# Split fp32r products for the expert keys and for two gathering blocks whose dots are fetched from memory, and for most value tiles

## The chip, the cores and the metric

The kernel runs on one core of one Trainium2 chip. The metric is the device time of a run in microseconds. Runs of the kernel before took 2939.55 to 2944.12 us, the median of three is 2941.18 us.

## What is computed

One encoder layer on 1024 tokens of width 1024: a mixer (a bidirectional gated recurrence and a convolution group between two projections), then a retrieval over 16384 single-neuron experts, then a last normalisation. The change concerns the retrieval:

```python
def _peer(h, wq, keys1, keys2, u_tab, v_tab):
    q = (h @ wq).reshape(nb, L, PEER_HEADS, PEER_DKEY)
    ...
    s1 = jnp.einsum('blhd,kd->blhk', q1, keys1)
    s2 = jnp.einsum('blhd,kd->blhk', q2, keys2)
    v1, i1 = lax.top_k(s1, PEER_TOPK)
    v2, i2 = lax.top_k(s2, PEER_TOPK)
    ...
    w = jax.nn.softmax(sc, axis=-1)
    ...
        u_sel = u_tab[ex]
        act = jax.nn.gelu(jnp.einsum('td,tjd->tj', hx, u_sel))
        coef = (wx * act)
        return jnp.einsum('tj,tjd->td', coef, v_tab[ex])
```

Each token has 8 heads x 16 = 128 experts e. For each it needs the dot of its h with row e of u, the gelu of that, times a softmax weight, times row e of V, summed. u and V have 16384 rows of 1024 floats (4 KB) each.

## The kernel before, in words

The program runs `step1`, `front`, `step4` (all up to the residual before the retrieval) and then `step6`, which is the retrieval and the ending. The token blocks of 128 are treated in two ways.

**Gathering blocks** 0 to 3 (`SPARSE = 4`). When a block is ranked (its 128 experts per token are known, `row[b]`), GpSimd orders one indirect DMA per expert place j (line 1657): 128 partitions each fetch their own 4 KB row of u or V into one of 8 ring slots (`RING`). `fetch(i)` waits until row i-8 has been taken. VectorE takes each: for u a product with h of that block that sums into `dot[b][:, j]` (line 2166; h stands in PSUM, `ph`), for V a multiply-add into `hB` (line 2180). The function `wanted(m)` gives the order, `sparse_by(n)` says how many rows are to be taken by tile n of u (in tenths per tile) and `sparse_by_v(n)` by tile n of V. The first 40 V rows of block 0 go another way, the side: fetched into two slots of their own and added on TensorE through a diagonal matrix (line 1752, `SIDE_ROWS`).

**Dense blocks** 4 to 7 (512 tokens). For these TensorE multiplies with all of u, tile by tile of 128 experts: `u_tile(n)` (line 1705) makes 8 plain fp32 products of 128x512, first for 16 tiles of the query weights (`QT`), then for 128 tiles of u. ScalarE copies or applies gelu (lines 1865, 1857) and stores to memory (`m.g`). Meanwhile VectorE ranks the blocks (`pick_step`, `ranked_key`), makes one-hot matrices (`one_hots`, lines 2139 to 2142), ScalarE their further parts (line 1910), TensorE multiplies them into a table of weights (line 1742), and ScalarE copies that out (line 1892) and stores it. Below this stretch, from the first query tile to the last tile of u, is called the u stage.

**V stage.** For 128 tiles of V, VectorE makes the product of g and the weights (`product_of`, lines 2198 and 2199), six tiles ahead, and TensorE multiplies 8 plain fp32 products per tile into all 8 banks of PSUM (line 1809). VectorE does the V rows of the gathering blocks in between. Then the sums are turned, the residual added, normalised and stored.

Every engine works through its own instructions in order, so a wait holds all that stands behind it. SP issues the loads of u and V tiles, weights and scores. Split products are used before already: `project` (lines 340, 341, 344) multiplies in fp32r with high and low parts of both sides, hi x hi, hi x lo, lo x hi; ScalarE rounds (line 324) and GpSimd subtracts (line 328).

## Time and profile before

| | |
|---|---|
| median of runs | 2941.18 us |
| profiled execution's own time | 2928.15 us, span 2926.1 us |
| TensorE busy | 2779.2 us (95%) |
| VectorE busy | 2238.6 us (77%) |
| GpSimd busy | 1263.6 us (43%) |
| ScalarE busy | 870.2 us (30%) |
| moved by DMA | 911.47 MB, of it 536.94 MB by the indirect gathers |

The profile comes from one execution. PE is TensorE's matmul part, PEld its loading of weights, DVE VectorE, ACT ScalarE, POOL GpSimd, SP the engine that issues loads. A "q" behind a name means the engine's sequencer. L1657 is line 1657 of the kernel. Time in which an engine waits is shown with what ended the wait. Matmuls overlap, so the mean time of one is longer than the distance between two; the distance is what counts. In a row of busy time by stretch the five engines stand as PE, PEld, DVE, ACT, POOL, each with its number of instructions.

### The profile page before, as it was taken

How to read it: one execution, taken by the hardware profiler on the slowest of the kernel's cores; microseconds unless marked ns; L12 is line 12 of the kernel's file. 1: busy time of each engine (PE TensorE's matmuls, PEld its weight loads, DVE VectorE, ACT ScalarE, POOL GpSimd, SP SyncE). 2: the span in 40 equal slices, each digit the busy share in tenths (PEclk: the TensorE clock that was granted, in tenths of full speed). 3: DMA queues.
4: the chain of work that ended last, by engine and by line, in shares of the span. 5: the costliest groups of instructions: out<-in, count | busy, mean ns of one | idle time of the engine just before them, and what ended most of it. 6: DMA issues, size and time to landing. Idle time of an engine off the chain costs nothing.

```text
span 2926.1 us, 31227 instructions
## 1 busy us (share of the span) xinstructions
PE 2779.2 (95%) x10124; PEld 1513.1 (52%) x10124; DVE 2238.6 (77%) x4600; ACT 870.2 (30%) x1733; POOL 1263.6 (43%) x1089
## 2 busy tenths in 40 slices
PE   6999889899999989999999999989999999999995
PEld 3677677787654434544454545534444444444442
DVE  5998566336799999999998968776776676677675
ACT  3223465333211014754664757800000000000004
POOL 1001111213354554444444445564666566656661
PEclk9999999999999999999999999999999999999997
DMA  5641101234499999999999999999999999999994
GB/s 204 252 173 40 48 30 47 85 135 123 161 406 388 388 379 338 399 383 369 393 360 365 369 400 414 416 407 390 405 402 405 407 397 405 398 402 401 402 393 180
DMA packets 284595, 911.47 MB, mean 311 GB/s; under 512 B 26001, under 2 KB 73361, under 8 KB 277137
## 3 DMA queue, kind: packets, MB, share of 16 engines
q0 software_dynamic: 147456, 536.94, 47.1%
q1 hardware_dynamic: 99632, 297.56, 27.1%
q10 hardware_dynamic: 37344, 74.98, 6.6%
q8 instruction: 81, 1.33, 0.2%
q14 instruction: 82, 0.66, 0.1%
HBM read 826.01 MB, written 83.36 MB: 311 GB/s over the span
## 4 chain that ended last, share of the span: by engine, by line
PE 23%; DMA 20%; DVE 19%; POOL 9%; issue 4%; DVEq 1%; ACT 1%; SPq 1%; ACTq 0%; PEldq 0%; POOLq 0%
DMA s_slot<-in_v,s_row 17%; PE s_pu L1705 16%; DVE s_slot L2166 10%; POOL s_slot L1657 9%; PE s_pw L1742 2%; DMA s_slot<-in_u,s_row 2%; DVE s_hB L2180 2%; PE s_ps L1752 1%; DMA s_wr<-s_w 1%; PE s_pu L340 1%; PE s_pu L341 1%; PE s_pu L344 1%; DVE pk_key L1364 1%; PE s_ps L1826 1%; DVE pk_key L1355 1%
## 5 line engine op out<-in xcount | busy, mean ns | idle before, releaser
L1705 PE MATMUL s_pu<-s_hn,s_ut 128*128 128x512 f32 x2304 | 1007.2, 593 | 4.3 <-ACT s_gst L1857 3.0
L1657 POOL DMA_INDIRECT s_slot<-in_v,s_row x512 | 638.5, 1247 | 372.6 <-DVE s_hB L2180 257.2
L2180 DVE SCALAR_TENSOR_TENSOR s_hB<-s_slot,s_dot,s_hB 128x1024 f32<-128x1024 f32 x469 | 593.3, 1284 | 254.2 <-DMA s_slot<-in_v,s_row 236.3
L1657 POOL DMA_INDIRECT s_slot<-in_u,s_row x512 | 504.6, 986 | 599.0 <-DVE s_slot L2166 521.1
L1705 PEld LDWEIGHTS s_pu<-s_hn,s_ut 128*128 128x128 f32 x2304 | 433.2, 190 | 530.0 <-issue 527.0
L2166 DVE SCALAR_TENSOR_TENSOR s_slot<-s_slot,s_ps 128x1024 f32<-128x1024 f32 x512 | 608.9, 1219 | 80.9 <-DMA s_slot<-in_u,s_row 60.3
L1809 PE MATMUL s_ps<-s_ct,s_vt 128*128 128x512 f32 x1024 | 460.3, 592 | 0.0
L1809 PEld LDWEIGHTS s_ps<-s_ct,s_vt 128*128 128x128 f32 x1024 | 194.6, 190 | 245.0 <-issue 245.0
L1910 ACT ACTIVATE s_hotw<-s_hot,s_rest 128x128 bf16<-128x128 bf16 x1024 | 308.5, 423 | 28.5 <-ACT s_gst L1857 23.7
L1989 ACT ACTIVATE s_sq<-y 128x512 f32<-128x512 f32 x16 | 8.9, 626 | 921.1 <-DVE y L2253 921.1
L1809 PE MATMUL s_pw<-s_ct,s_vt 128*128 128x512 f32 x512 | 246.0, 603 | 24.8 <-DMA s_vt<-in_v_tiles 15.6
L1809 PE MATMUL s_pu<-s_ct,s_vt 128*128 128x512 f32 x512 | 242.6, 596 | 0.0
L328 POOL TENSOR_TENSOR w_lo<-s2w_raw,w_hi 128x1024 fp32r<-128x1024 f32 x15 | 38.0, 2533 | 414.3 <-ACT w_hi L324 414.3
L340 PE MATMUL s_ps<-hn_hi,w_hi 128*128 128x512 f32 x464 | 189.0, 407 | 8.5 <-DVE hn_lo L280 8.0
L1857 ACT ACTIVATE s_gst<-s_pu 128x512 f32<-128x512 f32 x120 | 71.6, 597 | 403.7 <-PE s_pu L1705 403.1
L341 PE MATMUL s_ps<-hn_lo,w_hi 128*128 128x512 f32 x464 | 184.1, 397 | 0.0
L1809 PEld LDWEIGHTS s_pw<-s_ct,s_vt 128*128 128x128 f32 x512 | 97.5, 192 | 151.2 <-issue 129.3
L1809 PEld LDWEIGHTS s_pu<-s_ct,s_vt 128*128 128x128 f32 x512 | 98.7, 193 | 125.3 <-issue 125.3
L1028 DVE SCALAR_TENSOR_TENSOR s_work<-s_hp,cols,s_work 128x1024 f32<-128x1024 f32 x111 | 146.6, 1320 | 8.0 <-issue 0.4
L344 PE MATMUL s_ps<-hn_hi,w_lo 128*128 128x512 f32 x464 | 144.9, 394 | 0.0
L1892 ACT ACTIVATE s_wb<-s_pw 128x512 f32<-128x512 f32 x128 | 124.5, 1074 | 4.0 <-PE s_pw L1742 3.6
L1742 PEld LDWEIGHTS s_pw<-s_hotw,s_hot 128*128 128x128 bf16 x1536 | 93.1, 97 | 37.7 <-issue 37.3
(326 smaller groups left out, 2861.2 us busy)
## 6 DMA issues: line engine op xcount, KB each, us to landing
s_ut<-in_u_tiles SPq DMA_DIRECT2D x128, 512.0 KB, 7.4
s_vt<-in_v_tiles SPq DMA_DIRECT2D x32, 2048.0 KB, 16.9
s_g<-s_gst ACTq DMA_DIRECT2D x120, 256.0 KB, 7.0
s_w<-s_wb ACTq DMA_DIRECT2D x15, 2048.0 KB, 11.7
s_wr<-s_w SPq DMA_DIRECT2D x16, 1920.0 KB, 27.6
s_gr<-s_g SPq DMA_DIRECT2D x60, 512.0 KB, 26.7
s_ada<-in_ada SPq DMA_DIRECT2D x48, 512.0 KB, 6.2
s2w_raw<-in_w_in SPq DMA_DIRECT2D x26, 512.0 KB, 3.6
```

Source lines behind the costliest of these rows:

```text
L340: pe.matmul(out[:, c], w_hi[:, k, :], x_hi[:, h, k, :], start=(k == first), stop=False)
L341: pe.matmul(out[:, c], w_hi[:, k, :], x_lo[:, h, k, :], start=False, stop=False)
L344: mm = pe.matmul(out[:, c], w_lo[:, k, :], x_hi[:, h, k, :], start=False, stop=(k == last))
L1028: dve.scalar_tensor_tensor(dst, hp[:, k:k + T], cw[:, c, k:k + 1], work[:, :], ALU.mult, ALU.add)
L1657: pool.indirect_dma_start(out=slot[s][:, :], out_offset=None, in_=io[kind], in_offset=bass.IndirectOffsetOnAxis(ap=row[b][:, j:j + 1], axi ...
L1705: mm = pe.matmul(pu[:, n % 2, :], ut[n % UR][:, k, :], hn[:, k, :], start=(k == 0), stop=(k == DC - 1))
L1742: mm = pe.matmul(pw[:, unit % 2, j * P:(j + 1) * P], hot2[n % 2][:, q, :, t], hotw[n % 2][x][:, q, :, t], start=(x == 0), stop=(x == 2))
L1809: mm = pe.matmul(bank(c), vt[n // VG % VR][:, n % VG, c * P:(c + 1) * P], ct[:, n % CR, :], start=(n == 0), stop=(n == KEYS - 1))
L1892: act.activation(wb[chunk % 2][:, :, t:t + 4].rearrange("p k t -> p t k"), pw[:, unit % 2, :].rearrange("p (t k) -> p t k", t=4), ACT.Copy)\
L1910: o = act.activation(hotw[n % 2][1 + x][:, q, :, t], hot1[n % 2][:, q, :, t], ACT.Copy, scale=rest[:, x, 8 * r + i:8 * r + i + 1])
L2166: dve.scalar_tensor_tensor(s, s, 1.0, ph[:, :], ALU.mult, ALU.mult, accum_out=dot[b][:, j:j + 1]).then_inc(taken, 1)
L2180: dve.scalar_tensor_tensor(y, s, dot[b][:, j:j + 1], y, ALU.mult, ALU.add).then_inc(taken, 1)
```

## The change

1. **Dense tokens.** u and the query weights come as slices of 128x512 (one chunk k of the width for four tiles at once, `GROUP = 4`), 288 in all, through 5 buffers. ScalarE rounds a slice to `raw_hi` (3 buffers), and GpSimd (three of four slices) or VectorE (the fourth) subtracts to `raw_lo` in place. TensorE makes three fp32r products for each of four key banks. The dense tokens' h is kept as high and low parts too.
2. **Blocks 2 and 3** no longer gather u. With each slice of u, TensorE also multiplies their tokens (stationary) with all 512 keys of the slice, into two token banks. ScalarE copies these out through one buffer, `y_found`, and stores them in memory: 16384 dots for each token. When u is done, GpSimd fetches for each expert place the one dot per token by an indirect DMA of 4 bytes per partition (`find`), eight to a batch; ScalarE applies gelu to a batch, VectorE multiplies by the softmax weight.
3. **Gathering.** The order is now u of blocks 0 and 1, V of blocks 0 and 1, V of blocks 2 and 3: 768 rows in place of 984 and 40. `SIDE` and its TensorE work go. u products read h from SBUF (`hB`) and not from PSUM. One buffer for scores in place of two.
4. **V.** Of the 128 tiles 90 are split: ScalarE rounds the product and the tile, VectorE subtracts both, TensorE makes 24 fp32r products per tile. The other 38 stay plain.
5. The planner's numbers (`sparse_by`, `HOT_AT`) change, and h of the four gathering blocks is kept in two halves of 256 tokens (`ho_hi`, `ho_lo`, `project_gathering`).

```diff
+def project_gathering(pe, m, out, w_hi, w_lo, ks=range(DC)):
+
+    for k in ks:
+        x_hi, x_lo = m.ho_hi[:, :, k, :], m.ho_lo[:, :, k, :]
+        pe.matmul(pairs(out), w_hi[:, k, :], x_hi, start=(k == 0), stop=False)
+        pe.matmul(pairs(out), w_hi[:, k, :], x_lo, start=False, stop=False)
+        mm = pe.matmul(pairs(out), w_lo[:, k, :], x_hi, start=False, stop=(k == DC - 1))
     return mm
 
...
-RANKED = (0, 1, 2, 4, 5, 6, 3, 7)
+OWN_U = 2
+RANKED = (0, 1, 2, 4, 5, 6, 7, 3)
...
 RING = 8
-SIDE = 2
-SIDE_ROWS = 40
...
+GROUP = 4
+QG = QT // GROUP
+GROUPS = QG + KEYS // GROUP
+SLICES = DC * GROUPS
+RAW, ROUNDED = 5, 3
 KEPT = 8
...
-HOT_AT, HOT_TILES = (28, 54, 79, 101), (20, 20, 18, 17)
-SIDE_AT, SIDE_TILES = 26, 74
+HOT_AT, HOT_TILES = (28, 50, 72, 94), (19, 19, 19, 19)
+PLAIN_V = 120
+V_PARTS = [n for n in range(PLAIN_V) if n % 4]
+FOUND = 8
...
+def wanted(m):
+
+    if m < OWN_U * P:
+        return "u", m // P, m % P
+    j, b = divmod(m - OWN_U * P, 2)
+    return "v", 2 * (j // P) + b, j % P
+
+
+def slice_at(n):
+    return 2 * (n + QT)
+
+
+def split_by_dve(i):
+    return i % 4 == 0
 
...
-        tenths += 42 if t < 2 else 33 if t < 30 else 35 if t < 93 else 43 if t < 118 else 39
+        tenths += 22 if t < 0 else 37 if t < 28 else 25 if t < 93 else 42 if t < 114 else 50
...
+                for i in (slice_at(n), slice_at(n) + 1):
+                    if i >= RAW:
+                        sp.wait_ge(slice_done, i - RAW + 1)
+                    else:
+                        sp.wait_ge(wq.used, 2 * PH + (1 if i < 4 else 2))
+                    g, k = divmod(i, DC)
+                    sp.dma_start(raw[i % RAW][:, :], io["wq_groups"][g, k] if g < QG else io["u_groups"][g - QG, k])\
+                        .then_inc(raw_in[i % RAW], 16)
                 for i in range(MADE_PICKS, len(RANKED)):
...
+            def find(x, j):
+                if j == 0 and x >= 4:
+                    pool.wait_ge(found_used, x - 3)
+                e, c = found_column(x, j)
+                pool.indirect_dma_start(out=dot[OWN_U + e][:, c:c + 1], out_offset=None, in_=m.found[e],
+                                        in_offset=bass.IndirectOffsetOnAxis(ap=found_at[e][:, c:c + 1], axis=0))\
+                    .then_inc(found_in[x % 4], 16)
+
+            def remainder(i):
+                pool.wait_ge(raw_rounded, i + 1)
+                pool.tensor_tensor(raw_lo[i % RAW][:, :], raw[i % RAW][:, :], raw_hi[i % ROUNDED][:, :].bitcast(F32),
+                                   ALU.subtract).then_inc(raw_split[0], 1)
 
...
+                for i in (slice_at(n) + 2, slice_at(n) + 3):
+                    if i < SLICES and not split_by_dve(i):
+                        remainder(i)
+                    until = sparse_by(n + 1) if i % 2 else (asked + sparse_by(n + 1)) // 2
+                    for i in range(asked, until):
+                        fetch(i)
+                        asked = i + 1
+            for i in range(asked, V_FIRST):
+                fetch(i)
+            pool.wait_ge(y_stored, 16 * 2 * (KEYS // GROUP))
+            pool.wait_ge(found_ready, 2)
+            for x in range(2):
+                for j in range(FOUND):
+                    find(x, j)
+            for i in range(V_FIRST, SPARSE_OPS):
+                x, j = divmod(i - V_FIRST + 2 * FOUND, FOUND)
+                if x < 2 * P // FOUND:
+                    find(x, j)
                 fetch(i)
 
...
-            def u_tile(n):
-                i = n + QT
-                pe.wait_ge(u_in[n % UR], 16 * (i // UR + 1))
-                if i >= 2:
-                    pe.wait_ge(gelu_done, i - 1)
-                for k in range(DC):
-                    mm = pe.matmul(pu[:, n % 2, :], ut[n % UR][:, k, :], hn[:, k, :],
-                                   start=(k == 0), stop=(k == DC - 1))
-                mm.then_inc(u_done, 1)
+            def u_slice(i):
+                g, k = divmod(i, DC)
+                pe.wait_ge(raw_split[split_by_dve(i)], splits_before(i) + 1)
+                hi, lo = raw_hi[i % ROUNDED], raw_lo[i % RAW]
+                places = banks_of(g)
+                for kind, j in places:
+                    first, last = k == 0, k == DC - 1
+                    if first and g and (kind, j) in banks_of(g - 1):
+                        pe.wait_ge(emptied, emptied_before(g - 1) + banks_of(g - 1).index((kind, j)) + 1)
+                    if kind == "k":
+                        c = slice(j * P, (j + 1) * P)
+                        pe.matmul(key_bank[j], hi[:, c], m.hn_hi[:, 1, k, :], start=first, stop=False)
+                        pe.matmul(key_bank[j], hi[:, c], m.hn_lo[:, 1, k, :], start=False, stop=False)
+                        mm = pe.matmul(key_bank[j], lo[:, c], m.hn_hi[:, 1, k, :], start=False, stop=last)
+                    else:
+                        t = slice(j * P, (j + 1) * P)
+                        pe.matmul(token_bank[j], m.ho_hi[:, 1, k, t], hi[:, :], start=first, stop=False)
+                        pe.matmul(token_bank[j], m.ho_lo[:, 1, k, t], hi[:, :], start=False, stop=False)
+                        mm = pe.matmul(token_bank[j], m.ho_hi[:, 1, k, t], lo[:, :], start=False, stop=last)
+                    if (kind, j) == places[-1]:
+                        mm.then_inc(slice_done, 1)
+                    elif last:
+                        mm.then_inc(filled, 1)
...
+                if n in V_PARTS:
+                    x = V_PARTS.index(n)
+                    pe.wait_ge(v_split, x + 1)
+                    pe.wait_ge(ct_split, x + 1)
+                    hi, lo = v_hi[x % 2], v_lo[n // VG % VR]
+                    x_hi, x_lo = ct_hi[x % 4][:, :], ct_lo[:, n % CR, :]
+                    for c in range(DC):
+                        d = slice(c * P, (c + 1) * P)
+                        pe.matmul(bank(c), hi[:, d], x_hi, start=False, stop=False)
+                        pe.matmul(bank(c), hi[:, d], x_lo, start=False, stop=False)
+                        mm = pe.matmul(bank(c), lo[:, n % VG, d], x_hi, start=False, stop=False)
+                    mm.then_inc(v_done, 1)
+                    continue
...
+            def round_slice(i):
+                act.wait_ge(raw_in[i % RAW], 16 * (i // RAW + 1))
+                if i >= ROUNDED:
+                    act.wait_ge(slice_done, i - ROUNDED + 1)
+                act.activation(raw_hi[i % ROUNDED][:, :], raw[i % RAW][:, :], ACT.Copy).then_inc(raw_rounded, 1)
+
+            def empty_group(g):
+                t = g - QG
+                storing = []
+                for x, (kind, j) in enumerate(banks_of(g)):
+                    if x == len(banks_of(g)) - 1:
+                        act.wait_ge(slice_done, DC * (g + 1))
+                    else:
+                        act.wait_ge(filled, filled_before(g) + x + 1)
+                    if kind == "t":
+                        if 2 * t + j:
+                            act.wait_ge(y_stored, 16 * (2 * t + j))
+                        act.activation(y_found[:, :], token_bank[j], ACT.Copy).then_inc(emptied, 1)
+                        act.wait_ge(emptied, emptied_before(g) + x + 1)
+                        act.dma_start(m.found[j].rearrange("(t k) o -> t (k o)", t=P)[:, t * HALF:(t + 1) * HALF], y_found[:, :])\
+                           .then_inc(y_stored, 16)
+                    elif t < 0:
+                        if g:
+                            act.wait_ge(sd_made, GROUP * (g - 1) + j + 1)
+                        act.activation(qst[j][:, :], key_bank[j], ACT.Copy).then_inc(emptied, 1)
+                    elif GROUP * t + j >= KEYS - KEPT:
+                        act.activation(ct[:, (GROUP * t + j) % CR, :], key_bank[j], ACT.Gelu).then_inc(emptied, 1)
+                    else:
+                        if t:
+                            act.wait_ge(g_stored[j], 16 * t)
...
+            def round_product(x):
+                n = V_PARTS[x]
+                act.wait_ge(product, n + 1)
+                if x >= 4:
+                    act.wait_ge(v_done, V_PARTS[x - 4] + 1)
+                act.activation(ct_hi[x % 4][:, :], ct[:, n % CR, :], ACT.Copy).then_inc(ct_rounded, 1)
+
+            def round_tile(x):
+                n = V_PARTS[x]
+                act.wait_ge(v_in[n // VG % VR], 16 * (n // (VG * VR) + 1))
+                if x >= 2:
+                    act.wait_ge(v_done, V_PARTS[x - 2] + 1)
+                else:
+                    act.wait_ge(slice_done, SLICES)
+                act.activation(v_hi[x % 2][:, :], vt[n // VG % VR][:, n % VG, :], ACT.Copy).then_inc(v_rounded, 1)
+
+            def gelu_found(x):
+                e, c = found_column(x, 0)
+                act.wait_ge(found_in[x % 4], 16 * FOUND * (x // 4 + 1))
+                act.activation(dot[OWN_U + e][:, c:c + FOUND], dot[OWN_U + e][:, c:c + FOUND], ACT.Gelu).then_inc(found_used, 1)
+
...
-                    dve.scalar_tensor_tensor(s, s, 1.0, ph[:, :], ALU.mult, ALU.mult,
+                    dve.scalar_tensor_tensor(s, s, 1.0, hB[b][:, :], ALU.mult, ALU.mult,
...
+            def remainder(i):
+                dve.wait_ge(raw_rounded, i + 1)
+                dve.tensor_tensor(raw_lo[i % RAW][:, :], raw[i % RAW][:, :], raw_hi[i % ROUNDED][:, :].bitcast(F32),
+                                  ALU.subtract).then_inc(raw_split[1], 1)
+
```

## Rows read from the trace of the kernel before

**Rows 1.** Busy time by stretch: us, five engines in turn, clock, DMA share, GB/s
```profile
772.00:1966.00 1194.00, 1168.80 (x4140) 569.62 (x4140) 1059.61 (x2907) 552.58 (x1379) 582.97 (x583) 0.99 0.99 381
1966.00:2868.00 902.00, 885.47 (x2044) 390.19 (x2045) 640.73 (x686) 0.00 (x0) 559.58 (x441) 0.99 1.03 401
2868.00:2926.10 58.10, 24.43 (x69) 12.45 (x67) 30.42 (x39) 30.49 (x48) 0.57 (x1) 0.73 0.32 123
```

**Rows 2.** Chain of waits: shares of the span by engine; two pieces (start, us)
```profile
PE 23%; DMA 20%; DVE 19%; POOL 9%; issue 4%; DVEq 1%; ACT 1%; SPq 1%; ACTq 0%; PEldq 0%; POOLq 0%
...
1423.62 1.77 PE s_ps L1752 x4
...
1742.34 27.47 PE s_pu L1705 x64
```

**Rows 3.** Group of instructions on TensorE: shape, count, busy us, mean ns, idle before
```profile
L1705 PE MATMUL s_pu<-s_hn,s_ut 128*128 128x512 f32 x2304 | 1007.2, 593 | 4.3 <-ACT s_gst L1857 3.0 <-ACT s_hB L1952 1.1 <-DMA s_ut<-in_u_tiles 0.2
```

**Rows 4.** Instructions in order of time, TensorE in the query projection: start, us
```profile
689.98 0.39 PE L340 MATMUL s_pu<-hn_hi,w_hi 128*128 128x512 f32 x1
...
697.46 0.39 PE L340 MATMUL s_pu<-hn_hi,w_hi 128*128 128x512 f32 x1
```

**Rows 5.** Instructions in order of time, ScalarE in a tile with one-hots
```profile
1811.33 0.60 ACT L1857 ACTIVATE s_gst<-s_pu 128x512 f32<-128x512 f32 x1 [0.63 <-PE s_pu L1705]
...
1812.38 4.82 ACT L1910 ACTIVATE s_hotw<-s_hot,s_rest 128x128 bf16<-128x128 bf16 x16 [0.46 <-ACT s_gst L1857]
1817.08 1.94 ACT L1892 ACTIVATE s_wb<-s_pw 128x512 f32<-128x512 f32 x2
1819.63 0.60 ACT L1857 ACTIVATE s_gst<-s_pu 128x512 f32<-128x512 f32 x1 [0.61 <-PE s_pu L1705]
```

**Rows 6.** Groups on GpSimd in the V stage and in the u stage, and landings
```profile
L1657 POOL DMA_INDIRECT s_slot<-in_v,s_row x441 | 560.1, 1270 | 345.5 <-DVE s_hB L2180 255.0 <-issue 90.6
...
L1657 POOL DMA_INDIRECT s_slot<-in_u,s_row x512 | 504.6, 986 | 599.0 <-DVE s_slot L2166 521.1 <-issue 42.8 <-DVE s_row L2093 35.1
L1657 POOL DMA_INDIRECT s_slot<-in_v,s_row x71 | 78.3, 1103 | 27.0 <-issue 19.1 <-DVE s_slot L2166 4.8 <-DVE s_hB L2180 2.3
...
  issue: 90.6, 295
DMA to landing us min/median/max: 6.7/13.4/20.3
```

**Rows 7.** Instructions in order of time, V stage: GpSimd orders beside VectorE products
```profile
2398.79 3.67 DVE L2180 SCALAR_TENSOR_TENSOR s_hB<-s_slot,s_dot,s_hB 128x1024 f32<-128x1024 f32 x3 [0.19 <-issue]
...
2399.05 1.83 POOL L1657 DMA_INDIRECT s_slot<-in_v,s_row  x1 [0.30 <-issue]
...
2401.18 0.94 POOL L1657 DMA_INDIRECT s_slot<-in_v,s_row  x1 [0.30 <-issue]
```

**Rows 8.** Groups with two inputs in SBUF; and two VectorE products beside GpSimd
```profile
L2180 DVE SCALAR_TENSOR_TENSOR s_hB<-s_slot,s_dot,s_hB 128x1024 f32<-128x1024 f32 x469 | 593.3, 1284 | 254.2 <-DMA s_slot<-in_v,s_row 236.3 <-issue 16.5
L2199 DVE TENSOR_TENSOR s_ct<-s_gr,s_wr 128x480 f32<-128x480 f32 x120 | 78.0, 650 | 0.0
L328 POOL TENSOR_TENSOR w_lo<-s2w_raw,w_hi 128x1024 fp32r<-128x1024 f32 x15 | 38.0, 2533 | 414.3 <-ACT w_hi L324 414.3
...
259.89 6.74 DVE L1028 SCALAR_TENSOR_TENSOR s_work<-s_hp,cols,s_work 128x1024 f32<-128x1024 f32 x2
```

**Rows 9.** DMA queues from 772 to 900 us: packets, MB, share of 16 engines
```profile
q0 software_dynamic: 8573, 31.25, 63.0%
q10 hardware_dynamic: 7408, 3.68, 9.6%
```

**Rows 10.** DMA issues: count, KB each, median us to landing
```profile
s_ut<-in_u_tiles SPq DMA_DIRECT2D x128, 512.0 KB, 7.4
s_g<-s_gst ACTq DMA_DIRECT2D x120, 256.0 KB, 7.0
...
s_scores<-s_sc ACTq DMA_DIRECT2D x16, 256.0 KB, 2.3
```

422 lines of the change are left out of this document (222 added, 200 removed).

## The prediction

> **What bounds the kernel now.** I read the engines' shares on the page first (TensorE 95%), then busy time by stretch, then the chain of waits, then single instructions. The reader should see that the average hides four stages. By stretch [rows 1]: up to 772 us the front, the mixer and the first queries; 772 to 1966 (1194 us) the u stage, TensorE busy 1169; 1966 to 2868 (902 us) the V stage, TensorE busy 885; 58 us of ending. In both middle stages the DMA engines are full as well (share 0.99 and 1.03, 381 and 401 GB/s). The chain of waits [rows 2] says the same: row gathers, GpSimd, VectorE and TensorE share it. So a change must relieve TensorE and the gathers together, and neither may hand its work to an engine that becomes the next one.
>
> TensorE's prices. A plain fp32 product of 128x512 leaves two records, 1152 products giving x2304 [rows 3]; 64 records take 27.47 us [rows 2], so one product takes 0.858 us. The fp32r products of the query projection start 33 apart in 697.46 - 689.98 us [rows 4], 0.227 us each, so a split product (three of them) costs 0.680 us, 0.79 of the fp32 one.
>
> **TensorE in the u stage.** Before: 1152 products x 0.858 = 989 us; the side products 40 x 1.77 = 71 [rows 2]; the one-hot products 64 x 1.43 = 92 (a tile with them has a period of 1819.63 - 1811.33 = 8.30 us [rows 5], less 16 records x 0.429 = 6.87); the scores are what is left of the 1169 busy, 17; 25 us are idle [rows 1]. After: 32 query slices with 4 banks x 3 products = 384, and 256 slices of u with 6 banks (4 for the dense keys, 2 for blocks 2 and 3) x 3 = 4608. That is 4992 x 0.227 = 1132, plus 92 and 17: 1241 us, **+72 us**. The two extra token banks are what turns a saving into a cost. Two transposes of h fall away; the start needs the last remainder of the dense tokens instead, and I leave it at nothing.
>
> **TensorE in the V stage.** Before 1024 x 0.858 = 879. After 90 tiles split (24 x 0.227 = 5.44 us each, 490) and 38 plain (8 x 0.858 = 6.87, 261): 751 us, **-128 us**. If all the rest were hidden the kernel would win 56 us. The rest is the question.
>
> **GpSimd in the V stage.** This is my main term. The planner asks for 459 rows by the end of the u stage and there are 768, so 309 rows are left, where 442 were left before. Of these the first 53 are V rows of blocks 0 and 1. After them come 256 V rows of blocks 2 and 3, and each needs a dot that is fetched first by an indirect DMA of its own: 256 more of them. The plan hands out 309/126 = 2.45 rows per V tile. The ring lets the last of the 53 be asked for when VectorE has taken number 504, after 45/2.45 = 18 tiles, so after 18 x 5.86 + 9 (the gap at the start) = 114 us. From there GpSimd must issue 512 indirect DMAs one behind the other. One takes 1.270 us in this stage [rows 6] and 0.30 us passes between two (90.6 us over 295 [rows 6]): 1.57 us, 804 us in all. With the last landing (13.4 us [rows 6]) the stage takes 114 + 804 + 13 = **931 us**, 29 more than now, though TensorE needs only 751. A V tile then takes 2.45 x 2 x 1.57 = 7.7 us. The price varies: an indirect DMA that begins while VectorE has just begun a product with both inputs in SBUF takes 1.83 us, its neighbour 0.94 [rows 7]. The ends are 0.94 + 0.30 (512 x 1.24 = 635, stage 762) and 1.45 + 0.30 (896, stage 1023). I keep 1.57, as VectorE's load per unit of time is nearly unchanged: per V tile 2.45 x 1.28 + 0.83 for the product, and in 0.7 of the tiles the remainders of 512 and 1024 columns, 0.69 and 1.39 us by the 0.650 for 480 [rows 8], sum 5.4 us; over 7.7 us that is 70%, and now it is 641 of 902, 71% [rows 1].
>
> **DMA engines in the V stage.** Before 902 us x 401 GB/s = 362 MB. 133 rows of 0.524 MB fewer leave 292 MB, 728 us. No row shows a transfer of 4 bytes. The nearest short packets are the 512-byte ones of the scores: 9.6% of 128 us x 16 over 7408 packets [rows 9], 27 ns each; 256 x 144 x 27 ns / 16 = 61 us. The bound below is nothing, above it the time of a gather's own packets, 63.0% over 8573 [rows 9], 150 ns or 346 us. I take 61, stage 789 us: hidden behind GpSimd, but a floor for any hope that TensorE sets the end. The Trainium skill (DMA: Bandwidth & Descriptors, Bandwidth) gives a 4 KB transfer 0.68 us of engine time as its floor; 256 of these would be 174 us and make the DMA floor about 902 us. No run here shows it.
>
> **The rest of the u stage.** GpSimd orders 583 gathers in it now [rows 6] and 464 then (62 MB less; 17 MB of dots are stored), so the queues are looser. Four things are new on the path.
> 1. ScalarE rounds 288 slices, 0.6 us each, and empties a whole group of banks at once. With one store per bank it spends 1812.38 - 1811.33 = 1.05 us on each [rows 5]. The two token banks of a group go through one buffer, so the second copy waits until the store of the first has landed: 7.0 us for a store of this size now [rows 10], 2.3 us for the same size on quiet queues [rows 10]. ScalarE is in order; behind that wait stand 4.82 us of one-hot parts and 1.93 us of bank copies [rows 5], and behind them the rounding of the next slice. I follow one group from the start of its last slice: token bank 0 is full at 0.7 us and copied and sent at 1.5; bank 1 is copied from 8.5 to 9.1; the parts and copies end at 16.3, the rounding and its remainder at 18.2, while TensorE wants that slice at 4.08 + 1.43 + 8.16 + 1.43 = 15.1. So 3.1 us are lost with a store of 7 us, 0.5 with one of 3 us; I take 1.6 over 22 groups with one-hots and 0.6 us in 10 others: 40 us. Ends: 0 and 80.
> 2. GpSimd takes the remainders of 216 slices. 128x1024 took 2.53 us [rows 8], so half of it is 1.27. In the last 14 tiles five rows are planned per tile: 5 x 1.57 + 1.5 x 1.27 = 9.8 us against 8.16 of TensorE, 1.6 x 14 = 22 us. Ends 0 and 40. The 1.57 is the row of a product with both inputs in SBUF; the u products now read their h from PSUM and a gather's issue takes 0.986 beside them [rows 6], and the change moves h to SBUF.
> 3. GpSimd's subtraction and VectorE's two-input products exclude each other: two VectorE products beside two such subtractions took 6.74 us [rows 8], where one alone takes 1.28. VectorE is near full until tile 28 (busy 1060 of 1194 in the stage [rows 1]). I put 3 us here above today's idle, ends 0 and 30.
> 4. A slice is loaded four slices ahead, 16 us for a landing of 7.4 us with twice the bytes [rows 10]; covered. In the query groups it is 10.9 us less 2.5 for the splitting: covered, barely. If not, 32 slices x 1 us.
>
> The Trainium skill (GPSIMD Engine Reference, Specifications) says that GpSimd shares its SBUF interfaces with VectorE and contends with instructions of two SBUF inputs. That speaks against moving h to SBUF; without the rule the 22 us of point 2 would be 4, since 5 x 1.29 + 1.9 = 8.4. The traced 0.94 and 1.83 us agree with it.
>
> Sum: 1241 + 25 + 40 + 22 + 3 = **1331 us, +137**.
>
> **Total.** 2926.1 + 137 + 29 = 3092 us of span. Its own time is 2928.15, 2 more than the span; the median of the runs, 2941, lies 13 above that. So 3092 + 2 + 13 = 3107; since the ends of the four small terms reach further down in common than up, I say 3100.
>
> **The rivals.**
> A. GpSimd sets the V stage, as above: 3000 to 3180 us. For it: 512 orders in a row on one engine, a count that no wait can shrink.
> B. All is covered (the other side, faster). The price of an indirect DMA near 0.94 us makes GpSimd's stage 762, so the DMA floor of 789 decides; the u stage is 1241 + 25. Span 2926 + 72 - 113 = 2885, so 2900 to 2930. It decides where the mean price falls below (789 - 127)/512 = 1.29 us with the gap. Against it: VectorE's duty does not fall.
> C. Between: price 1.40 with the gap, u stage 1290: 114 + 717 + 13 = 844, so 2926 + 96 - 58 + 15 = 2979; 2945 to 3000.
> D. The chain load, round, subtract, multiply runs late in the whole u stage, because GpSimd's waits for ring slots stand ahead of subtractions: each of 144 pairs of slices 1 us late, +144 and less of point 1: 3180 to 3260. For it: the in-order queue. Against: windows of 8 us.
> E. The change doesn't do what it says, if a split product doesn't hold 0.227 us with weights changing at each: every 0.01 us is 50 + 22 us. Against it: the query stage changes weights at each one too.
>
> **How the numbers follow.** A 0.55, D 0.14 with E in it, C 0.14, B 0.14, and 0.03 for chance sums near no change. Likeliest: A, 3100 us. Leaving out the outer part of B and D the range is 2915 to 3210. A measurement can tell about 0.2%, 6 us: slower 0.80 (A, D and most of C), same 0.05, faster 0.15.
>
> **What would show it.** Right: TensorE in the V stage idle before weight loads, with waits on VectorE's products; GpSimd there without waits on ring slots, at some 1.5 us per order; V tiles of 7 to 8 us. In the u stage ScalarE's idle time before the second token copy ended by a DMA landing, once per group. Wrong: V tiles of 5.9 us; GpSimd waiting for VectorE; a u stage under 1280 us. The price of the 4-byte fetches and of the product with h in SBUF are the two that no row shows and that could undo it.

## The result, and the profile after

The changed kernel takes **3193 us** (median of 4 runs, 3185 to 3200) against 2940 us before: ratio **1.086**, 95% interval 1.083 to 1.089. The prediction was 3100 us with a range of 2915 to 3210 and 0.80 for slower, so time and sign lie inside it; the time is 3% above the forecast. The profiled execution took 3185 us, its span is 3183.2 us.

First the busy time by stretch, with the columns of [rows 1]: the u stage, two pieces of its end, and the V stage.

```profile
771.00:2186.00 1415.00, 1290.60 (x6668) 1048.47 (x6668) 1222.14 (x2625) 747.84 (x1685) 935.96 (x682) 0.97 0.84 294
1860.00:2162.00 302.00, 272.32 (x1395) 215.53 (x1394) 236.37 (x184) 149.38 (x341) 236.95 (x177) 0.99 0.93 339
2162.00:2186.00 24.00, 0.42 (x2) 0.00 (x1) 11.61 (x14) 0.98 (x2) 7.89 (x9) 0.57 1.03 409
2186.00:3140.00 954.00, 829.83 (x2768) 545.64 (x2768) 642.56 (x784) 147.44 (x216) 612.45 (x557) 0.91 0.84 301
```

The u stage grew from 1194 to 1415 us, the V stage from 902 to 954, the ending shrank from 58 to 43. In the u stage TensorE is busy 1291 us where its products at full clock make 1241; the other 124 us it idles, 24 of them in the gap ahead of V, where it waits for VectorE's first products. In the V stage it is busy 830 us where the products make 751, and idles 124 us. The DMA engines, full in [rows 1], stand at 0.84. VectorE is busy 162 us more in the u stage than before, though it works on 457 gathered rows there (256 of u, 201 of V) and not on 532 (512 and 20).

What TensorE waited for in the u stage, with total, times and longest:

```profile
PE s_ps L1795 <- DVE s_raw_lo L2309: 37.7, 15, 5.0
PE s_ps L1795 <- POOL s_raw_lo L1739: 32.4, 31, 2.3
PE s_pu L1790 <- DVE s_raw_lo L2309: 17.0, 4, 8.9
PE s_pu L1790 <- POOL s_raw_lo L1739: 8.5, 1, 8.5
PE s_ps L1795 <- ACT s_y_found L1953: 8.5, 8, 3.5
```

These are late remainders of slices, VectorE's before GpSimd's; the token banks' buffer is the last row. ScalarE's own wait for that buffer, over the whole run, is this one:

```profile
ACT s_y_found L1953 <- DMA s_found<-s_y_found: 47.5, 17, 6.9
```

The groups of VectorE in the u stage and of GpSimd in the V stage (shape, count, busy us, mean ns):

```profile
L2291 DVE SCALAR_TENSOR_TENSOR s_slot<-s_slot,s_hB 128x1024 f32<-128x1024 f32 x256 | 365.7, 1452 | 26.3 <-DMA s_slot<-in_u,s_row 13.0 <-issue 1.5
L2267 DVE TENSOR_TENSOR s_hot<-s_iota,s_keyT 128x1024 bf16<-128x1024 bf16 x64 | 63.5, 993 | 0.0
...
L1725 POOL DMA_INDIRECT s_slot<-in_v,s_row x301 | 348.9, 1159 | 224.9 <-DVE s_hB L2305 137.9 <-issue 78.6 <-DVE s_hB L2302 8.5
L1733 POOL DMA_INDIRECT s_dot<-s_found,s_found_at x256 | 263.5, 1029 | 78.0 <-issue 78.0
```

The product of a u row with h takes 1.452 us where it took 1.219, the one-hots 0.99 where they took 0.68. In the V stage GpSimd makes 557 orders of 1.10 us with 0.30 between, and waits 138 us for ring slots. TensorE's only long wait there for another engine is this one:

```profile
PE s_pw L1892 <- DVE s_v_lo L2321: 28.2, 9, 11.6
```

Last, a look at what TensorE does in a bad stretch of the V stage: three windows, and single products (start, us, the idle time before).

```profile
2364.00:2384.00 20.00, 19.55 (x75) 13.57 (x74) 17.05 (x20) 3.35 (x6) 15.12 (x17) 1.00 0.74 228
2384.00:2404.00 20.00, 10.59 (x25) 5.72 (x24) 10.32 (x15) 1.57 (x2) 13.91 (x14) 0.66 0.76 255
2404.00:2424.00 20.00, 19.05 (x65) 12.84 (x64) 13.02 (x15) 4.32 (x6) 11.22 (x10) 0.91 1.00 356
```

```profile
2386.49 0.39 PE L1893 MATMUL s_pw<-s_ct_lo,s_v_hi 128*128 128x512 f32 x1 [0.60 <-issue]
2387.91 0.39 PE L1894 MATMUL s_pw<-s_ct_hi,s_v_lo 128*128 128x512 f32 x1 [1.03 <-issue]
2388.64 0.49 PE L1892 MATMUL s_pu<-s_ct_hi,s_v_hi 128*128 128x512 f32 x1 [0.34 <-issue]
2390.03 0.40 PE L1893 MATMUL s_pu<-s_ct_lo,s_v_hi 128*128 128x512 f32 x1 [0.91 <-issue]
2391.45 0.59 PE L1894 MATMUL s_pu<-s_ct_hi,s_v_lo 128*128 128x512 f32 x1 [1.02 <-issue]
```

TensorE stands between products of one tile, whose operands have long been there, and "issue" says that it waited for nothing that the profile shows. Starts lie about 0.7 or 1.4 us apart. From 2391 on the products take 0.6 us: the granted clock has gone to the lower level, 1.2 GHz, after the stalls. In the whole V stage such gaps make 93 of the 124 idle us. I count as a cluster three or more of them within 3.5 us of each other; the V stage after has 12 clusters with 78 us of idle time in them.

### The profile page after: what moved, and what is told of

Same layout as the page of the kernel before. It is cut to its first block, busy times and chain, and to the rows that moved or that the text cites. A ratio compares the mean times of both kernels' runs of the same rounds, so it can differ in the third digit from the quotient of the medians.

```text
span 3183.2 us, 38967 instructions
## 1 busy us (share of the span) xinstructions
PE 2833.8 (89%) x13340; PEld 2137.2 (67%) x13340; DVE 2409.8 (76%) x4422; ACT 1210.5 (38%) x2253; POOL 1667.3 (52%) x1305
## 4 chain that ended last, share of the span: by engine, by line
PE 31%; DVE 16%; POOL 8%; issue 7%; ACT 6%; DMA 4%; DVEq 3%; another core or an unknown queue 3%; ACTq 1%; PEldq 0%; POOLq 0%
DVE s_slot L2291 6%; POOL s_slot L1725 5%; PE s_ps L1900 3%; ACT s_hotw L2015 3%; DMA s_found<-s_y_found 2%; POOL s_raw_lo L1739 2%; PE s_ps L1894 2%; PE s_ps L1893 2%; PE s_ps L1892 2%; PE s_ps L1795 2%; PE s_pw L1900 2%; PE s_pu L1900 1%; PE s_ps L1797 1%; PE s_ps L1796 1%
## 5 line engine op out<-in xcount | busy, mean ns | idle before, releaser
L1739 POOL TENSOR_TENSOR s_raw_lo<-s_raw,s_raw_hi 128x512 fp32r<-128x512 f32 x216 | 317.7, 1471 | 359.1 <-ACT s_raw_hi L1940 356.6
L2291 DVE SCALAR_TENSOR_TENSOR s_slot<-s_slot,s_hB 128x1024 f32<-128x1024 f32 x256 | 365.7, 1452 | 26.3 <-DMA s_slot<-in_u,s_row 13.0
L1733 POOL DMA_INDIRECT s_dot<-s_found,s_found_at x256 | 263.5, 1029 | 78.0 <-issue 78.0
L1795 PE MATMUL s_ps<-s_raw_hi,ho_hi 128*128 128x512 f32 x512 | 213.3, 417 | 79.8 <-DVE s_raw_lo L2309 37.7
L1790 PE MATMUL s_pu<-hn_hi,s_raw_hi 128*128 128x512 f32 x576 | 232.7, 404 | 25.5 <-DVE s_raw_lo L2309 17.0
L1791 PE MATMUL s_pu<-hn_lo,s_raw_hi 128*128 128x512 f32 x576 | 229.8, 399 | 0.0
L1792 PE MATMUL s_pu<-hn_hi,s_raw_lo 128*128 128x512 f32 x576 | 229.7, 399 | 0.0
L1790 PE MATMUL s_ps<-hn_hi,s_raw_hi 128*128 128x512 f32 x576 | 227.4, 395 | 0.1
L1791 PE MATMUL s_ps<-hn_lo,s_raw_hi 128*128 128x512 f32 x576 | 226.7, 394 | 0.0
L1792 PE MATMUL s_ps<-hn_hi,s_raw_lo 128*128 128x512 f32 x576 | 225.8, 392 | 0.0
```

The lines of the kernel that those rows point to most:

```text
L1733: pool.indirect_dma_start(out=dot[OWN_U + e][:, c:c + 1], out_offset=None, in_=m.found[e], in_offset=bass.IndirectOffsetOnAxis(ap=found_at ...
L1739: pool.tensor_tensor(raw_lo[i % RAW][:, :], raw[i % RAW][:, :], raw_hi[i % ROUNDED][:, :].bitcast(F32), ALU.subtract).then_inc(raw_split[0 ...
L1790: pe.matmul(key_bank[j], hi[:, c], m.hn_hi[:, 1, k, :], start=first, stop=False)
L1791: pe.matmul(key_bank[j], hi[:, c], m.hn_lo[:, 1, k, :], start=False, stop=False)
L1792: mm = pe.matmul(key_bank[j], lo[:, c], m.hn_hi[:, 1, k, :], start=False, stop=last)
L1795: pe.matmul(token_bank[j], m.ho_hi[:, 1, k, t], hi[:, :], start=first, stop=False)
```

## The experiments

All kernels are edits of the kernel after; of each edit the telling lines are shown, and "..." stands for the others. "u" and "V" below are the two stages in the profiled execution. Five of the kernels leave the u stage as it is, and it took 1406 to 1411 us in them, 1415 in the kernel after; three leave the V stage as it is, and it took 949 to 952, 954 after.

### What sets the V stage

**No fetches.** Lines 1733 to 1735 go; the dots of blocks 2 and 3 are made zero.

```
-                pool.indirect_dma_start(out=dot[OWN_U + e][:, c:c + 1], out_offset=None, in_=m.found[e],
...
-                act.wait_ge(found_in[x % 4], 16 * FOUND * (x // 4 + 1))
+                act.wait_ge(found_ready, 2)
```

> The 256 fetches of dots are left out; the dots of blocks 2 and 3 are zero instead, everything else is as in the kernel after. Theory 1 (my prediction's main term: the orders of GpSimd, one behind the other, set the V stage, which took 956 us): GpSimd is left with 309 orders, 309 x 1.40 = 433 us, TensorE sets the stage with 751 us of products at the full clock plus some 30 us: V stage 780 to 800, total about 3030 us. Theory 2 (splitting V, the in-order chain load, round on ScalarE, subtract on VectorE, multiply, sets it): the stage stays at 900 or more, total 3140 to 3193. TensorE's gaps of 0.7 to 2.8 us between single matmuls (some 50 us in 400 us of the stage): gone if the fetches cause them, still there if the split products do.

Measured: 2985 us, ratio 1.017 (1.014 to 1.020). The V stage by itself:

```profile
2186.00:2942.00 756.00, 754.27 (x2768) 521.41 (x2768) 637.21 (x783) 147.38 (x216) 417.67 (x301) 1.00 0.98 379
```

756 us, TensorE busy 754 at full clock, no cluster. So the 256 fetches of 4 bytes cost 198 us of 954, and splitting V does what it promised as long as nothing else is late: 754 against the 751 of the sum. Theory 2 is out; theory 1 had put the stage at 780 to 800, too long.

**Fetches from the start of the stage.** Each batch has its own semaphore, and the fetches are spread evenly.

```
...
-            for i in range(V_FIRST, SPARSE_OPS):
-                x, j = divmod(i - V_FIRST + 2 * FOUND, FOUND)
-                if x < 2 * P // FOUND:
-                    find(x, j)
+            found, last = 0, V_FIRST + 2 * P - 4 * FOUND
+            for i in range(asked, SPARSE_OPS):
+                while found < 2 * P and found * (last - asked) < 2 * P * (i + 1 - asked):
+                    find(*divmod(found, FOUND))
+                    found += 1
                 fetch(i)
...
```

> The same 256 fetches of dots, but spread over the V stage from its beginning, each batch of 8 with a semaphore of its own, so that no batch waits for an earlier one to be used. Theory 1 (count of orders): the 118 us at the start of the stage, in which GpSimd issues 53 orders only, come free; 565 orders x 1.40 = 791 us plus 40 of start and last landing: V stage 830 to 870, total 3090 to 3110. Theory 1b (not the count but the latency of each batch, which ScalarE waits for ahead of rounding the next V tiles: 153 us of such waits): these waits are gone as well, and VectorE's late products with them; the stage then goes towards TensorE's 751 to 800, total 3030 to 3060. Theory 2 (the splitting chain): 3180 or more.

Measured: 3065 us, ratio 1.044 (1.041 to 1.048).

```profile
2188.00:3029.00 841.00, 784.03 (x2769) 537.65 (x2770) 645.55 (x782) 147.63 (x216) 620.00 (x560) 0.96 0.93 341
```

841 us, as theory 1 said of the stage; the total is 25 us below its range. GpSimd's orders stand 1.435 us apart with 15 us of longer pauses in all: it works from end to end. ScalarE's 153 us of waits for fetched batches are gone as well, and the stage still doesn't come near the 751 to 800 of theory 1b. There is no cluster either, so this run doesn't say how much of the 113 us comes from the earlier start and how much from the missing stalls.

**V not split**, in the kernel after:

```
-V_PARTS = [n for n in range(PLAIN_V) if n % 4]
+V_PARTS = []
...
```

> V is not split: all 128 tiles are plain fp32 products of 8 x 0.858 = 6.87 us, 879 us in all instead of 751; the u stage and the fetches are as in the kernel after. Theory 1 (GpSimd's orders set the stage): the first find moves from 118 to about 135 us and the rest stays, V stage 940 to 980, total 3175 to 3215. Theory 2 (the chain that splits V sets it): the stage becomes shorter, TensorE's 879 plus 30, total about 3145. Theory 3 (the split is worth what it saves on TensorE): V stage 956 + 128, total about 3320.

Measured: 3127 us, ratio 1.066 (1.061 to 1.070), **faster** than with V split.

```profile
2186.00:3069.00 883.00, 880.90 (x2048) 389.50 (x2048) 476.06 (x591) 6.68 (x32) 662.33 (x557) 1.00 0.89 323
```

No theory had that number; theory 2's total comes nearest. But its chain isn't all that the row shows: TensorE does 128 us more work than the split needs and the stage is 71 us shorter; it never stops, and the granted clock is 1.00. VectorE and ScalarE lose the splitting too, 167 and 141 us, so this run alone doesn't say which of the two shortens the stage. The next one does. After the first fetch GpSimd's orders follow at 1.49 us without one wait for the ring. My theory 1 had taken the stage of 954 us for GpSimd's floor. It isn't: in the kernel after the 512 orders from the first fetch on take 1.07 us each with 0.30 between, 705 us, and the last one ends 796 us after the first began.

**Filling.** Four products with a zero matrix ahead of each split tile from tile 20 on, 68 us of added work.

```
+                if n >= 20 and n in V_PARTS:
+                    for c in range(4):
+                        pe.matmul(bank(c), m.zero[:, :], m.turn[:, :].unsqueeze(1).broadcast_to([P, 4, P]), start=False, stop=False)
...
```

> Added work: ahead of each split V tile from tile 20 on TensorE makes four fp32r products of 512 columns with a zero matrix, 75 x 4 x 0.227 = 68 us. They fall where TensorE idles now (124 us of the stage). Theory 1 with the clock (TensorE waits for others, and each wait is followed by a stretch at the lower clock level, 81 us in the stage): the granted clock of the stage rises from 0.91 to 0.96 or more and the time stays or falls, total 3170 to 3200. Rival (TensorE and its weight loads are the bound in this stage, or the clock falls for another reason than the idle gaps): the clock stays near 0.91 and the stage takes 50 to 70 us more, total 3240 to 3265.

Measured: 3098 us, ratio 1.057 (1.054 to 1.060): 3% faster than the kernel after, with more work in it.

```profile
2189.00:3055.00 866.00, 834.07 (x3068) 581.47 (x3068) 642.99 (x782) 147.15 (x216) 607.09 (x557) 0.98 0.91 331
```

More than either theory said. The splitting is still there; the clock is 0.98, the real products take 834 - 68 = 766 us instead of 830, and there is no cluster. Orders start 1.395 us apart from the first fetch on; 118 + 512 x 1.395 + some 34 for the last landing and the last tiles is the 866. That is GpSimd's floor with fetches that begin late.

**Both, early fetches and filling**: the edits of the second and the fourth run together.

> The two edits together that gained most one by one: the fetches spread over the V stage from its start (V stage 841 us), and four products with a zero matrix ahead of each split V tile from tile 20 on (V stage 866 us, granted clock 0.98 there). Theory 1 (GpSimd's orders are the bound, and the low clock only cost time while it was TensorE that GpSimd's queue waited for through the ring): with the early fetches GpSimd waits only 15 us for ring slots, so filling gains no more than that: V stage 825 to 845, total 3050 to 3070. Theory 2 (the low clock costs by itself, both gains add up): V stage 760 to 790, total about 2990.

Measured: 3170 us, ratio 1.080 (1.073 to 1.086), worse than either alone. Both theories miss.

```profile
2186.00:3124.00 938.00, 872.44 (x3068) 589.67 (x3068) 642.52 (x784) 147.26 (x216) 618.04 (x560) 0.96 0.86 306
```

The clusters are back, 11 of them with 53 us. So filling doesn't prevent them by itself, and the gain of the run before can't be put down to the clock alone: there the stalls were gone too.

### What sets the u stage

**One store per group.** The copy of token bank 0 isn't stored; block 2 then fetches the dots of block 3.

```
+                        if not j:
+                            continue
...
```

> The store of token bank 0 is left out in every group (block 2 then fetches the dots of block 3), so the second copy into the one buffer waits for nothing. Theory 1 (point 1 of the prediction: that wait holds up the rounding of the next slice, 40 us in the u stage, ends 0 and 80): the u stage (1415 us with its gap) falls by 40 us or more, total 3110 to 3155. Theory 2 (the trace after: ScalarE waits 41 to 47 us for these landings, but only some 8 to 20 us of TensorE's idle time follow from it; the rest goes by late remainders): the u stage falls by 5 to 20 us, total 3170 to 3190. Half the stores and their descriptors go as well, 8.4 MB.

Measured: 3156 us, ratio 1.076 (1.070 to 1.082).

```profile
776.00:2161.00 1385.00, 1283.45 (x6668) 1048.43 (x6668) 1216.04 (x2624) 748.94 (x1685) 936.89 (x682) 0.97 0.84 295
```

The u stage takes 21 to 30 us less than with both stores: between the theories. ScalarE has no wait for a store any more, and TensorE's 8.5 us behind the token copy are gone; its waits for remainders fall by some 9 us and its busy time by 7.

**The share of the remainders.** After, `split_by_dve` gives VectorE each fourth slice. Two runs change that line, a third gives VectorE all slices (and has the early fetches, which act in the V stage alone).

```
-    return i % 4 == 0
+    return i < 1
```

> All slices but the first have their remainder from GpSimd; before, each fourth was VectorE's. Theory 1 (VectorE, 86% busy in the u stage with products of 1.45 us and one-hots ahead of its remainder in its queue, gives that remainder late: 55 us of TensorE's waits, and the low clock behind them): the u stage falls by 40 to 70 us, total 3120 to 3150. Theory 2 (GpSimd's in-order queue is the tight one, point 2 of the prediction: 72 more subtractions of 1.47 us on an engine whose remainders come late already): the waits only move to GpSimd's remainder; the u stage is the same or up to 40 us longer, total 3190 to 3235.

```
-    return i % 4 == 0
+    return i % 2 == 0
```

> Each second slice's remainder from VectorE instead of each fourth, so that GpSimd has 144 and VectorE 144. With all of them on GpSimd the u stage was 18 us longer (1433). Theory 1 (both queues are tight, the best share lies between): within 20 us of the kernel after, total 3170 to 3210. Theory 2 (VectorE, 86% busy, is the later one): 72 remainders of 0.89 more, 64 us, and each late behind products and one-hots: u stage 1450 to 1490, total 3225 to 3270. Theory 3 (GpSimd is): total 3140 to 3165.

```
-    return i % 4 == 0
+    return True
```

> Two edits: all remainders of slices from VectorE (GpSimd makes none), and the fetches of dots spread over the V stage from its start, which alone made that stage 841 us. The u stage is read by itself. Its product with h took 1.521 us with 288 subtractions on GpSimd, 1.452 with 216, 1.314 with 144, and the stage 1433, 1415, 1349. Theory 1 (GpSimd's subtraction beside VectorE is what both pay for; h in SBUF alone costs little): product at 1.25 or below, VectorE's busy time no higher than 1200 although it makes 144 remainders of 0.8 more, u stage 1290 to 1330, total 2960 to 3010. Theory 2 (VectorE's in-order queue is late as soon as it has all remainders; the best share is in the middle): u stage 1350 to 1400, total 3030 to 3080. Theory 3 (the gathers beside it make the product long, not the subtractions): product stays at 1.30 or more, VectorE above 1260, u stage 1370 or more.

The product with h in the runs with 288, 144 and no subtractions on GpSimd (with 216 it stands above):

```profile
L2291 DVE SCALAR_TENSOR_TENSOR s_slot<-s_slot,s_hB 128x1024 f32<-128x1024 f32 x256 | 383.4, 1521 | 33.3 <-DMA s_slot<-in_u,s_row 20.8 <-issue 0.4
```

```profile
L2291 DVE SCALAR_TENSOR_TENSOR s_slot<-s_slot,s_hB 128x1024 f32<-128x1024 f32 x256 | 330.1, 1314 | 21.7 <-DMA s_slot<-in_u,s_row 8.5 <-issue 1.2
```

```profile
L2284 DVE SCALAR_TENSOR_TENSOR s_slot<-s_slot,s_hB 128x1024 f32<-128x1024 f32 x256 | 306.7, 1224 | 17.9 <-DMA s_slot<-in_u,s_row 4.9 <-issue 0.9
L2302 DVE TENSOR_TENSOR s_raw_lo<-s_raw,s_raw_hi 128x512 fp32r<-128x512 f32 x288 | 188.7, 688 | 62.3 <-ACT s_raw_hi L1933 55.5
L2260 DVE TENSOR_TENSOR s_hot<-s_iota,s_keyT 128x1024 bf16<-128x1024 bf16 x64 | 43.8, 684 | 0.0
```

And their u stages, in the same order:

```profile
779.00:2212.00 1433.00, 1304.38 (x6668) 1043.36 (x6667) 1246.06 (x2552) 745.87 (x1685) 1027.06 (x753) 0.98 0.84 290
```

```profile
779.00:2128.00 1349.00, 1272.75 (x6669) 1038.89 (x6668) 1176.17 (x2696) 747.63 (x1685) 798.72 (x610) 0.98 0.86 307
```

```profile
770.00:2117.00 1347.00, 1272.06 (x6668) 1040.40 (x6668) 1148.98 (x2853) 747.90 (x1687) 566.98 (x465) 0.98 0.85 307
```

Totals: 3204 us, ratio 1.090 (1.084 to 1.096); 3116 us, 1.061 (1.056 to 1.066); 3004 us, **1.026** (1.023 to 1.029). VectorE's busy time **falls** as it takes more remainders, from 1246 to 1149 us: a subtraction costs it 0.69 us when GpSimd makes none, and every one that GpSimd makes lengthens VectorE's products and one-hots. The stage falls by 57 to 66 us at the half share and then no further; TensorE, busy 1272 of 1347 us, is near its bound there. GpSimd has 72 subtractions fewer at the half share, so its own queue is looser too, and the 57 to 66 us can't be put down to the cheaper products alone. So in the first run theory 2 holds; the second misses all three ranges, below even that of theory 3, which comes nearest; and theory 1 of the last run is right on the prices and 17 us too low on the stage. That kernel is the fastest whole one of the study, and still slower than the kernel before.

**No token banks, own u rows in all four blocks**, at the pace of the kernel before, u and V split:

```
-OWN_U = 2
+OWN_U = 4
...
-        tenths += 22 if t < 0 else 37 if t < 28 else 25 if t < 93 else 42 if t < 114 else 50
+        tenths += 42 if t < 2 else 33 if t < 30 else 35 if t < 93 else 43 if t < 118 else 39
...
```

> One part alone: u and V are split as in the kernel after, but all four gathering blocks fetch their u rows and make their own dots, at the pace of the kernel before (535 of 1024 rows by the end of the u stage, 489 in the V stage). No token banks, no stores and no fetches of dots. Theory 1 (VectorE sets the u stage then: 1222 us busy now, less 256 products of 1.53 and 201 sums of 1.46, plus 512 and 23 of them: 1354 us): u stage about 1400, V stage 920 to 950, total 3110 to 3180; the token banks were not what made the kernel slow. Theory 2 (my sum: two token banks are what turns a saving into a cost, 349 us of TensorE; GpSimd's 535 orders x 1.67 and 216 remainders x 1.57 give 1232): u stage 1235 to 1260, V stage 850 to 900, total about 2950. TensorE's own 892 us would allow a stage below 1000.

Measured: 3218 us, ratio 1.096 (1.090 to 1.101), u 1435 and V 966 us. My sum's reading (theory 2) falls: without the 349 us of token products, and with the u rows gathered in their place, the u stage is not shorter at all. It is theory 1's side, and slower than its 3180. The rows of the two stages, of TensorE's waits in the u stage, and of VectorE's products and GpSimd's orders:

```profile
772.00:2207.00 1435.00, 1045.62 (x5132) 819.96 (x5132) 1308.09 (x2953) 708.53 (x1623) 1051.10 (x758) 0.88 0.86 305
2207.00:3173.00 966.00, 815.11 (x2768) 553.66 (x2768) 848.12 (x929) 142.74 (x182) 581.68 (x482) 0.93 1.02 396
...
PE s_pu L1782 <- DVE s_raw_lo L2298: 260.1, 56, 14.7
PE s_pu L1782 <- POOL s_raw_lo L1741: 92.8, 59, 11.6
...
L2280 DVE SCALAR_TENSOR_TENSOR s_slot<-s_slot,s_hB 128x1024 f32<-128x1024 f32 x512 | 727.8, 1455 | 73.8 <-DMA s_slot<-in_u,s_row 54.7 <-issue 2.7
L1727 POOL DMA_INDIRECT s_slot<-in_u,s_row x512 | 702.9, 1373 | 173.1 <-issue 111.9 <-DVE s_slot L2280 41.4 <-DVE s_row L2207 12.2
```

VectorE is busy 91%, TensorE waits for late remainders, and the granted clock is 0.88; its 892 us of products show as 1046 us busy. In the V stage, without fetches, the DMA engines are at 1.02 and 396 GB/s, full as in [rows 1]: the split V gains nothing there.

**The same with h in PSUM.** The two banks that are free without token banks hold h of the block in work.

```
+                        dve.tensor_copy(py[:, :], hB[b][:, :])
...
-                    dve.scalar_tensor_tensor(s, s, 1.0, hB[b][:, :], ALU.mult, ALU.mult,
+                    dve.scalar_tensor_tensor(s, s, 1.0, py[:, :], ALU.mult, ALU.mult,
```

> The kernel with own u rows in all four gathering blocks and no token banks (u stage 1435 us, VectorE 91% busy, its 512 products with h 1.455 us each, GpSimd's gathers 1.37 us each), with one edit: h of the block in work is copied to the two PSUM banks that the token banks would have had, and the product reads it there. Theory 1 (h in SBUF is what costs: contention of GpSimd with two-input products of VectorE on SBUF): product near 1.22 us and gather near 1.0 us as in the kernel before, VectorE 1308 - 512 x 0.23 = 1190 us, fewer late remainders; u stage 1280 to 1330, total 3080 to 3120. Theory 2 (the products are longer because of GpSimd's subtractions and the slices' traffic, whatever h is read from): product stays above 1.4 us, total 3200 to 3220.

Measured: 3103 us, ratio 1.057 (1.054 to 1.061).

```profile
771.00:2089.00 1318.00, 1019.75 (x5132) 807.31 (x5132) 1179.18 (x2959) 708.93 (x1623) 838.10 (x758) 0.89 0.90 332
...
PE s_pu L1782 <- DVE s_raw_lo L2305: 214.9, 56, 14.2
PE s_pu L1782 <- POOL s_raw_lo L1741: 42.0, 36, 11.6
```

```profile
L2287 DVE SCALAR_TENSOR_TENSOR s_slot<-s_slot,s_ps 128x1024 f32<-128x1024 f32 x512 | 607.9, 1219 | 79.6 <-DMA s_slot<-in_u,s_row 58.4 <-issue 4.3
...
L1727 POOL DMA_INDIRECT s_slot<-in_u,s_row x512 | 517.9, 1012 | 181.3 <-issue 93.7 <-DVE s_slot L2287 64.4 <-DVE s_row L2209 12.2
```

Product 1.219 us, to the nanosecond that of the kernel before, although GpSimd still makes its 215 subtractions; gather order 1.012 us where it took 1.373; u stage 117 us shorter: theory 1, and inside its ranges. So in these runs a product pays for GpSimd's work only if both of its inputs lie in SBUF.

**No token banks and no fetches**, with two gathering blocks as after:

```
-            return [("k", j) for j in range(GROUP)] if g < QG else [("t", 0)] + [("k", j) for j in range(GROUP)] + [("t", 1)]
+            return [("k", j) for j in range(GROUP)]
...
```

> The token banks of blocks 2 and 3 are left out with their copies and stores, and so are the fetches of dots (the dots of these blocks are zero); gathers, splitting and everything else as in the kernel after. TensorE's u stage loses 256 x 6 x 0.227 = 349 us of products. Theory 1 (VectorE with 1216 busy us, and GpSimd's and ScalarE's chain of rounding and subtracting, stand right behind TensorE in the u stage): the stage falls from 1406 in the run without fetches to 1250 or 1300 only, and the granted clock falls below 0.92; total 2830 to 2890. Theory 2 (TensorE alone sets the stage): 1060 to 1110, total about 2680.

Measured: 2922 us, ratio 0.995 (0.994 to 0.997).

```profile
770.00:2120.00 1350.00, 1031.67 (x5133) 817.03 (x5133) 1224.40 (x2630) 708.70 (x1621) 931.79 (x682) 0.88 0.84 296
...
PE s_pu L1786 <- DVE s_raw_lo L2305: 204.0, 47, 9.4
```

349 us of TensorE's work shorten the stage by 56. Theory 1's side, and worse than it said: VectorE's 1224 us with their waits stand right behind TensorE. Even with all the work for blocks 2 and 3's dots left out, the kernel only draws level with the one before.

## Why the prediction was right, and where its steps failed

**Right as a whole**: slower, and for the greater part through the u stage, +221 us, where the prediction had +137; the V stage adds 52 and the ending gives 15 back. Two steps have their own proof. The price of the split product (0.227 us three times; rival E) holds: 754 us without fetches against 751. The DMA price of the fetches was put at 61 us of 16 engines: share times length is 0.84 x 954 = 801 us after and 0.98 x 756 = 741 without them, 60 us; in the run with early fetches, 0.93 x 841, it is 41. (The shares have two digits, which leaves some 5 us open in each.) The Trainium skill (DMA: Bandwidth & Descriptors, Bandwidth) has 0.68 us for a 4 KB transfer, the smallest of its table; taken 256 times that is an estimate of 174 us. A fetch here moves 512 bytes beside other transfers, and these rows are against adding that figure up for it.

**TensorE's clock was missing.** The sum took every product at full speed, as [rows 1] show it at 0.99. After, busy time is above the products by 1291 - 1241 = 50 us in u and 830 - 751 = 79 in V, **129 us** that no step had. Not all of it is the clock. The trace grants the lower level, 1.2 GHz, for 63 us of the u stage up to 2162 and for 174 us of the V stage, and TensorE is busy in 55 and 115 of them; half of that, 27 and 58 us, 85 in all, is what the clock costs. Much of the rest comes of the stalls themselves: a product that stands alone counts as 0.39 us busy, in a row each adds 0.227. The Trainium skill (TensorE: Matmul & The Clock Gate, Part 1) says that the clock halves after idleness; the trace agrees, with products of 0.6 us from 2391 on. A step that says "TensorE will idle here" has to price that as well.

**The u stage, +221 for +137.** The work term, +72, stands; beside it come 99 us more of idle time and the 50 above, where the sum had 65. The single effects below overlap and don't add up to that. Of the four small terms:
1. The buffer of the token banks: 40 us, measured 21 to 30 with half the stores gone too. ScalarE waited for a landing 17 times in 32 groups, not once in each. The chain that I followed doesn't add up either: 9.1 + 4.82 + 1.93 is 15.9 and not 16.3, and with a store of 3 us the remainder comes at about 14, before the 15.1 at which TensorE wants it, so nothing is lost and not 0.5.
2. GpSimd in the last 14 tiles: 22 us. They took 136 us (row below) for 114 us of products, 22 more; 15 of these are TensorE's waits for GpSimd's remainders, 15 times.
3. **The exclusion of GpSimd's subtraction and VectorE's two-input products: 3 us, ends 0 and 30. This is the mis-sized step.** With half of the subtractions on VectorE and not a fourth the stage is 57 to 66 us shorter, and moving h alone to PSUM makes it 117 us shorter in the kernel with 512 products. The mechanism and the row for it [rows 8] were there, but I counted only the waits and not that 256 products and 192 one-hot instructions would each take 0.2 to 0.3 us longer on an engine that was 89% busy.
4. Slice loads were covered: 10 us of ScalarE's waits.

```profile
2026.00:2162.00 136.00, 120.15 (x507) 92.86 (x505) 102.05 (x71) 30.87 (x51) 118.08 (x89) 1.00 0.97 350
```

To these comes the gap ahead of the V stage, 24 us, where before it was about 9.

The Trainium skill's rule on shared SBUF interfaces (GPSIMD Engine Reference, Specifications), which I priced for GpSimd's side and hardly for VectorE's, was the right one, and in these runs both sides pay: VectorE's product takes 1.219 us with h in PSUM, 1.224 with h in SBUF and no subtractions on GpSimd, 1.452 with h in SBUF and 216 of them, and GpSimd's order 1.012 us with h in PSUM and 1.373 with h in SBUF.

**The V stage, +52 for +29.** That GpSimd's orders are the floor of this stage is what the runs show: 756 us without the fetches, 841 with early ones, 866 with late ones and TensorE kept busy. But that floor lies below the 902 us of the kernel before; the orders eat most of what splitting saves, and don't make the stage longer. The last 88 us, from 866 to 954, come of TensorE's stalls and its clock, which the prediction did not have. Its 804 us agree with the 796 measured by accident. The price is 1.38 us and not 1.57 (an order takes 1.07, not 1.27), 705 us, with which my sum would have given a stage of 832; the other 91 are pauses, in which GpSimd waits for ring slots while VectorE waits for a rounding that waits for TensorE, which stalls and runs at the lower clock. Rival C had the price, 1.40, but not the pauses. Of the signs that I had named, the 7 to 8 us per V tile came (954/128 = 7.5). GpSimd without waits on ring slots does not hold for this kernel; it nearly does for those with early fetches or filling. And TensorE's waits for VectorE are 28 of its 124 idle us, not the bulk of them.

**"The two extra token banks are what turns a saving into a cost"** was wrong. Taking them away with gathers put back made the kernel slower (3218 us): it frees TensorE, and VectorE with 1308 us becomes the bound. The clearest comparison is the run with h in PSUM, whose gathers and products are as before: 1318 us of u stage for 1194, though TensorE has 892 us of products for 1169, and it waits 257 us for late remainders. So what turns the saving into a cost is the splitting itself, as it is arranged here: 288 roundings, 288 subtractions and a chain load, round, subtract, multiply, on engines that [rows 1] show at 89%, 46% and 49% and of which two slow each other. Whether more buffers for slices (5 raw, 3 rounded) would hide the chain, no run tests.

**Open**: the cause of the clusters, below. No run takes them away alone.

## What to carry to other kernels

When work leaves a bound engine, add up the next three engines first, with the prices that hold once they share ports; an engine at 89% is the next bound. Put elementwise work that runs beside VectorE's two-input SBUF products on VectorE itself, or move one input to PSUM: here either made its busy time fall. And price TensorE's idle time twice where it comes in short pieces: once as the wait, once for the products at the lower clock behind it; a slower kind of product that keeps it busy and needs no splitting can be the faster choice (883 against 954 us).
